# The last stage of a decoder layer on one core: row sums a tile ahead, variance on ScalarE, expert rows landed in 8 KB pieces, fewer rows on TensorE for the first and the last tile

## The chip, the core and the metric

The kernel runs on one core of one Trainium2 chip. The core has a TensorE (PE), a VectorE (DVE), a ScalarE (ACT), a GpSimd (POOL) and a SyncE (SP), which run their own instruction lists side by side and wait for one another through semaphores. The metric is the device time of one launch in microseconds, the median of several runs.

## The reference, cut to what matters

The reference is one decoder layer over 512 prompt tokens and 64 sample tokens (576 in all), with 1024 channels: attention and a gated convolution, a mixture of 64 experts of which each token uses 6, and a per-layer embedding term. The change touches only its last two steps, the sum of a token's six expert rows and the second layer norm:

```
y = jax.ops.segment_sum(yb * row_w[:, None].astype(yb.dtype), row_tok, num_segments=t + 1)
...
h = layer_norm(DN_ALPHA * h + ffn.reshape(n, s, D_MODEL) + ple, lw['ln2_g'], lw['ln2_b'])

def layer_norm(x, g, b):
    mu = jnp.mean(xf, axis=-1, keepdims=True)
    xc = xf - mu
    var = jnp.mean(xc * xc, axis=-1, keepdims=True)
    return (xc * lax.rsqrt(var + LN_EPS) * g + b).astype(x.dtype)
```

## The kernel before

Everything is float32. The 576 tokens are five tiles: tiles 0 to 3 hold 128 prompt tokens each, on 128 partitions, and tile 4 holds the 64 sample tokens. After the projections, attention and routing, a loop over 32 pairs of experts (L1336 to L1344) runs gate, up and down products on PE while SP loads the next pair's weights, each 1 MB load in pieces of 8 KB (L553). Each pass writes its weighted rows to a table in HBM, `expert_rows`, where token i has eight row slots of 4 KB, the first six in use (POOL L695). The shared expert, the residual and the embedding term are already in `res`, in SBUF.

The last stage starts when POOL signals `all_out`, after the last rows have been written.

- **SP** (L613 to L623) issues five loads, `part[t] <- expert_rows` (L617), one for each tile in the order 4, 0, 1, 2, 3 (`LAST_ORDER`); a token's six rows are 24 KB in one run. Then it waits for each tile's `y_done` and stores the tile (L622). All these are on SP's one queue.
- **PE** (L1346 to L1356) sums the first `N_ON_PE = 4` of the six rows of each tile by multiplying them with an identity matrix: four products for each half of 512 channels, accumulated in PSUM. Each product is two matmul instructions in the trace, so a tile is 16 of them.
- **DVE** (L1886 to L1905) waits for the tile's rows, adds the other two rows to `res` (L1893), waits for PE's sum (`part_sum`, L1895) and adds it (L1897), takes the statistics of the two halves (L1900) and joins them (L1902). Then, before it turns to the next tile, it normalises the tile before: `normalise` (L1575 to L1584) takes a reciprocal and makes two passes over the tile, (x - mean) * gain (L1580) and * 1/std + shift (L1583). The second one signals `y_done`.
- **ACT** takes only the square root of the variance (`root`, L846), on a 128x1 column.

The order is written out by hand: nothing plans or reorders it. `normalise` and `root` serve the first layer norm too, and are not changed.

Of the kernel before, what the change touches and what calls it, by code (L numbers as in the profile page):

```python
# [7 lines left out]
F32 = mybir.dt.float32  # L8
# [4 lines left out]
ALU = mybir.AluOpType  # L13
ACT = mybir.ActivationFunctionType
AX = mybir.AxisListType

P = 128
D = 1024
# [5 lines left out]
NT = (T + P - 1) // P  # L24
# [7 lines left out]
NE, TOPK, NGRP, TOPG = 64, 6, 8, 4  # L32
# [26 lines left out]
GATE_SLOT = (1, 0, 0, 0)  # L59
TPAIR = 3  # L60
LAST_ORDER = (NT - 1, *range(NT - 1))
N_ON_PE = 4

def pack_constants():
# [43 lines left out]
def decoder_step(nc, x_prompt, x_sample, p_prompt, p_sample, win_k, win_v, conv_state, w_in, sinks,  # L109
# [4 lines left out]
    with ctx:  # L114
        base0 = (nc.sbuf_base + 31) // 32 * 32

        def at(name, shape, dt, off):
            return nc.alloc_sbuf_tensor_at(name, shape, dt, offset=base0 + off)
# [53 lines left out]
        ident = sm("ident", [P, P], F32)  # L172
# [19 lines left out]
        eps = sm("eps", [P, 1], F32)  # L192
        mv = sm("mv", [P, NT, 2], F32)
        rstd = sm("rstd", [P, NT], F32)
# [7 lines left out]
        stats = at("stats", [P, NT, 4, 6], F32, o_stats)  # L202
# [36 lines left out]
        o_w2, o_w1, o_w0, o_x = 20480, 69632, 118784, 167936  # L239

        res = at("res", [P, NT, D], F32, o_a)
# [68 lines left out]
        g2b2 = at("g2b2", [P, 2, D], F32, o_x)  # L310
# [17 lines left out]
        x2_d = nc.dram_tensor("x2_rows", [T, D], F32)  # L328

        rows_d = nc.dram_tensor("expert_rows", [T * 8 + 1, D], F32)  # L330
        part = [at(f"part{t}", [P, TOPK, D], F32, o_w2 + 4 * TOPK * D * t) for t in range(NT)]

        def sum_banks(n):

            return (proj, att)[n // 2 % 2][:, n % 2 * 2:n % 2 * 2 + 2, :]
# [26 lines left out]
        std_ready, var_ready, x2_ready, x2_out = (sem(n) for n in ("std_ready", "var_ready", "x2_ready", "x2_out"))  # L362
# [15 lines left out]
        part_in = [sem(f"part_in{t}") for t in range(NT)]  # L378
        y_free, all_out, part_sum, part_added = (sem(n) for n in ("y_free", "all_out", "part_sum", "part_added"))
        y_done, y_out = sem("y_done"), sem("y_out")  # L380
# [12 lines left out]
        def ntok(t):  # L393
            return P if t < NT - 1 else NS
# [55 lines left out]
        def _(sp):  # L450
# [14 lines left out]
            for n in range(1, G_AO):  # L465
# [3 lines left out]
                else:  # L469
                    j = Q_AT.index(n)  # L470
# [31 lines left out]
            with sp.Fori(0, 2) as it:  # L502
                for i in range(6):
                    c0 = (COL_CC, COL_CH, COL_CB)[i % 3] + i // 3 * GW
# [32 lines left out]
            for t in range(NT):  # L537
                w = ntok(t)
# [75 lines left out]
            for t in LAST_ORDER:  # L614
                w = ntok(t)
                rows = rows_d[t * P * 8:(t * P + w) * 8, :].rearrange("(p j) n -> p j n", j=8)
                sp.dma_start(part[t][0:w, :, :], rows[:, 0:TOPK, :]).then_inc(part_in[t], 16)  # L617
            for n, t in enumerate(LAST_ORDER):
                w = ntok(t)
                sp.wait_ge(y_done, n + 1)  # L620
# [87 lines left out]
        def _(act):  # L708
# [8 lines left out]
            for n, (t, c) in enumerate(QUADS):  # L717
                act.wait_ge(tr_x, n + 1)
                w = ntok(t)
# [26 lines left out]
            for n in range(N_STEP + 3):  # L746
                if n < N_STEP:
                    j, blk, pair = at_step(n)
                    r = n % 2
                    act.wait_ge(nm_ready, n + 1)  # L750
                    for e in range(2):
                        nc.scalar.activation(s_p[n % 4][:, e, :], s_p[n % 4][:, e, :], ACT.Exp,
                                             bias=nm[:, r, e:e + 1], accum_out=sm_p[:, r, e:e + 1])
# [16 lines left out]
                if n >= 4 and n % 2 == 0:  # L770
                    b = n // 2 - 2
                    j, blk, _ = at_step(2 * b)
# [70 lines left out]
            def root(t):  # L843

                w = ntok(t)
                nc.scalar.activation(rstd[0:w, t:t + 1], mv[0:w, t, 1:2], ACT.Sqrt, bias=eps[0:w, :]).then_inc(std_ready, 1)  # L846
# [5 lines left out]
            for t in range(NT):  # L852
                w = ntok(t)
                for c in range(2):
                    n = 2 * t + c
# [3 lines left out]
                for c in range(2):  # L859
                    n = 2 * t + c  # L860
# [80 lines left out]
                passes(it + 5)  # L941

            for n, t in enumerate(LAST_ORDER):
                act.wait_ge(var_ready, NT + n + 1)
                root(t)

        @block.tensor
        def _(pe):
# [25 lines left out]
            for n, (t, c) in enumerate(QUADS):  # L975
# [3 lines left out]
                w = ntok(t)  # L979
                for j in range(4):  # L980
                    k = 4 * c + j
                    last = nc.tensor.transpose(att[:, n % 4, j * P:j * P + w], x_tok[0:w, t, k * P:(k + 1) * P],
                                               ident[0:w, 0:w])
# [7 lines left out]
            for t in range(NT):  # L991
                w = ntok(t)
# [3 lines left out]
            for b in range(NB_S):  # L996
                last = nc.tensor.transpose(att[:, 2 + b // 4, b % 4 * P:(b % 4 + 1) * P], cache_k[:, b, :], ident[:, :])
# [33 lines left out]
            for n in range(N_STEP + 2):  # L1031
                if n < 24:
                    fill(2)
                if 24 <= n < N_STEP:
# [6 lines left out]
                    for e in range(2):  # L1041
                        r = slice(e * HD, (e + 1) * HD)
                        o = att[r, b % 2, 256:256 + KEYS_S]
                        nc.tensor.matmul(o[:, 0:WIN], q_smp[r, b, :], cache_kt[r, b, :], start=True, stop=True)
                        last = nc.tensor.matmul(o[:, WIN:KEYS_S], q_smp[r, b, :], k_t[r, WIN + SEQ:], start=True, stop=True)
                    last.then_inc(sl_ready, 1)
                if n < N_STEP:
                    j, blk, pair = at_step(n)
# [5 lines left out]
                    for e in range(2):  # L1054
                        r = slice(e * HD, (e + 1) * HD)
# [32 lines left out]
            for b in range(NB_S):  # L1088
                for e in range(2):
                    r = slice(e * HD, (e + 1) * HD)  # L1090
# [48 lines left out]
            for t in range(NT):  # L1139
                w = ntok(t)  # L1140
# [23 lines left out]
            for t in range(NT):  # L1164
                w = ntok(t)
# [180 lines left out]
            for n, t in enumerate(LAST_ORDER):  # L1346
                w = ntok(t)
                pe.wait_ge(part_in[t], 16)
                if n >= 4:
                    pe.wait_ge(part_added, n - 3)  # L1350
                for half in range(2):
                    for j in range(N_ON_PE):
                        last = nc.tensor.matmul(sum_banks(n)[0:w, half, :], ident[0:w, 0:w],  # L1353
                                                part[t][0:w, j, half * 512:(half + 1) * 512],
                                                start=(j == 0), stop=(j == N_ON_PE - 1))
                last.then_inc(part_sum, 1)  # L1356

# [1 line left out]
        def _(dve):  # L1360
# [214 lines left out]
            def normalise(t, gb):  # L1575

                w = ntok(t)
                nc.vector.reciprocal(rstd[0:w, t:t + 1], rstd[0:w, t:t + 1])
                dve.drain()
                nc.vector.scalar_tensor_tensor(res[0:w, t, :], res[0:w, t, :], mv[0:w, t, 0:1], gb[0:w, 0, :],  # L1580
                                               ALU.subtract, ALU.mult)
                dve.drain()
                return nc.vector.scalar_tensor_tensor(res[0:w, t, :], res[0:w, t, :], rstd[0:w, t:t + 1], gb[0:w, 1, :],  # L1583
                                                      ALU.mult, ALU.add)  # L1584
# [299 lines left out]
                passes(it + 5)  # L1884

            dve.wait_ge(ld_ln2, 32)  # L1886
            for n in range(NT + 1):
                if n < NT:
                    t = LAST_ORDER[n]
                    w = ntok(t)  # L1890
                    dve.wait_ge(part_in[t], 16)
                    for j in range(N_ON_PE, TOPK):
                        nc.vector.tensor_tensor(res[0:w, t, :], res[0:w, t, :], part[t][0:w, j, :], ALU.add)  # L1893
                        dve.drain()
                    dve.wait_ge(part_sum, n + 1)  # L1895
                    r = res[0:w, t, :].rearrange("p (a n) -> p a n", a=2)
                    nc.vector.tensor_tensor(r, r, sum_banks(n)[0:w, :, :], ALU.add).then_inc(part_added, 1)  # L1897
                    dve.drain()
                    for c in range(2):
                        nc.vector.bn_stats(stats[0:w, t, c, :], res[0:w, t, c * 512:(c + 1) * 512])  # L1900
                    dve.drain()
                    nc.vector.bn_aggr(mv[0:w, t, :], stats[0:w, t, 0:2, :]).then_inc(var_ready, 1)  # L1902
                if n >= 1:
                    dve.wait_ge(std_ready, NT + n)
                    normalise(LAST_ORDER[n - 1], g2b2).then_inc(y_done, 1)  # L1905

# [24 lines left out]
```

## Time and profile before

| | us |
|---|---|
| median of 3 runs (1363.01 to 1366.27) | 1364.27 |
| the profiled execution's own time | 1364.62 |
| its span, first to last record | 1362.8 |
| PE busy in the span | 1252.1 (92%) |
| DVE busy | 499.0 (37%) |
| last expert pass's last product on PE ends | 1288.2 |
| SP issues the first load of the last stage | 1293.67 |
| DVE's last instruction ends | 1359.73 |

The times in a trace are microseconds from the start of the span. "PE" rows are matmuls, "PEld" their weight loads. A share of busy time is an average over stages: PE is busy for 92% of the span, but in the last 75 us the work passes from DMA to PE to DVE, and only what is late in that stretch matters to this change. The granted clock is TensorE's: 1.00 is 2.4 GHz and 0.50 is 1.2 GHz.

### The profile page before, as it was taken

The page shows a single profiled execution, that of the slowest core. Times are in us where ns is not written, and L with a number is a line of the kernel's source. Part 1 is how long each engine was busy: PE and PEld are TensorE (multiplying, and loading weights), DVE is VectorE, ACT ScalarE, POOL GpSimd, SP SyncE. Part 2 cuts the span into 40 slices and gives each one's busy share as a digit, 9 for nine tenths or more (in the row PEclk, how much of TensorE's full clock was granted, in tenths as well). Part 3 has the DMA queues.
Part 4 walks back from the last instruction along what each step waited for, and adds up shares of the span by engine and source line. Part 5 has one row for each costly group of instructions (what it writes and reads, how often), then busy time and mean ns, then how long its engine had stood idle before and what let it go on. Part 6 is the DMA issues. An engine that isn't in the chain of part 4 may idle for free.

```text
span 1362.8 us, 23702 instructions
## 1 busy us (share of the span) xinstructions
PE 1252.1 (92%) x8911; PEld 1008.6 (74%) x8912; DVE 499.0 (37%) x1090; ACT 298.9 (22%) x547; POOL 129.9 (10%) x200
## 2 busy tenths in 40 slices
PE   6999997999999999999889899989998799999675
PEld 6988876999999999998867667656665466666422
DVE  3455672324444233576862222111111111111128
ACT  3344452212212222224001111111111111111100
POOL 0200000000000000004000111111221121112100
PEclk8999996999999999999899999999999999999968
DMA  8211210222222231433346988999999999999592
GB/s 259 78 52 63 59 36 19 74 94 76 79 92 64 93 98 66 170 104 139 124 197 260 415 318 329 419 421 421 420 419 412 416 414 411 414 408 416 208 376 110
DMA packets 98318, 308.08 MB, mean 226 GB/s; under 512 B 11370, under 2 KB 62402, under 8 KB 73092
## 3 DMA queue, kind: packets, MB, share of 16 engines
q1 hardware_dynamic: 84692, 275.20, 53.0%
q0 software_dynamic: 12480, 28.60, 5.4%
q10 hardware_dynamic: 1088, 3.47, 0.7%
q8 instruction: 40, 0.66, 0.2%
q14 instruction: 18, 0.15, 0.0%
HBM read 295.95 MB, written 26.94 MB: 237 GB/s over the span
## 4 chain that ended last, share of the span: by engine, by line
PE 53%; DMA 35%; DVE 8%; DVEq 1%; issue 1%; ACT 1%; SPq 0%; ACTq 0%; POOLq 0%
DMA w_exp<-in_w_e_down_dram 33%; PE proj L963 31%; PE proj L1124 4%; PE att L1256 3%; PE att L1312 2%; PE att L1133 2%; PE proj L1329 2%; PE proj L1353 2%; PE att L1056 1%; DMA pg_raw<-in_w_ple_gate_dram 1%; PE att L1018 1%; PE att L1124 1%; PE att L1069 1%; DMA part<-expert_rows 1%; PE att L1092 0%
## 5 line engine op out<-in xcount | busy, mean ns | idle before, releaser
L1312 PE MATMUL att<-w_exp,xt 128*64 128x256 f32 x2560 | 289.4, 383 | 23.2 <-issue 11.3
L1312 PEld LDWEIGHTS att<-w_exp,xt 128*64 128x64 f32 x2560 | 221.0, 138 | 100.1 <-issue 46.1
L963 PE MATMUL proj<-h_hi,w_hi 128*128 128x288 f32 x800 | 178.3, 305 | 4.8 <-DVE h_lo L1365 4.8
L963 PE MATMUL proj<-h_lo,w_hi 128*128 128x288 f32 x800 | 171.9, 297 | 0.0
L963 PE MATMUL proj<-h_hi,w_lo 128*128 128x288 f32 x800 | 171.8, 297 | 0.0
L1329 PE MATMUL proj<-w_exp,ht_e 128*64 128x512 f32 x640 | 149.2, 607 | 11.2 <-DMA w_exp<-in_w_e_down_dram 6.6
L963 PEld LDWEIGHTS proj<-h_hi,w_hi 128*128 128x128 f32 x800 | 128.4, 190 | 20.2 <-issue 15.2
L963 PEld LDWEIGHTS proj<-h_lo,w_hi 128*128 128x128 f32 x800 | 129.7, 190 | 0.0
L963 PEld LDWEIGHTS proj<-h_hi,w_lo 128*128 128x128 f32 x800 | 129.4, 190 | 0.0
L432 DVE TENSOR_TENSOR w_lo<-w_raw,w_hi 128x2048 fp32r<-128x2048 f32 x33 | 75.6, 2291 | 100.1 <-ACT w_hi L422 94.7
L1329 PEld LDWEIGHTS proj<-w_exp,ht_e 128*64 128x64 f32 x640 | 51.1, 139 | 81.8 <-issue 80.0
L422 ACT ACTIVATE w_hi<-w_raw 128x2048 fp32r<-128x2048 f32 x33 | 63.0, 1909 | 97.6 <-PE proj L963 80.8
L1857 DVE TENSOR_SCALAR ysb<-proj,tabw 128x512 f32 x40 | 30.0, 751 | 144.1 <-PE proj L1329 144.1
L1848 DVE TENSOR_TENSOR sg<-sg,att 128x256 f32<-128x256 f32 x40 | 16.8, 421 | 121.7 <-ACT sg L918 121.7
L1852 DVE TENSOR_TENSOR h_e<-sg,att 128x256 f32<-128x256 f32 x40 | 16.8, 421 | 120.0 <-PE att L1312 119.8
L925 ACT ACTIVATE ysb<-proj,tabw 128x512 f32 x40 | 27.5, 687 | 145.2 <-PE proj L1329 145.2
L963 PE MATMUL proj<-mix_hi,w_hi 128*128 128x288 f32 x256 | 55.7, 300 | 1.7 <-DVE mix_lo L1483 1.7
L963 PE MATMUL proj<-mix_hi,w_lo 128*128 128x288 f32 x256 | 55.3, 298 | 0.0
L963 PE MATMUL proj<-mix_lo,w_hi 128*128 128x288 f32 x256 | 55.3, 298 | 0.0
L920 ACT ACTIVATE ht_e<-att 128x256 f32<-128x256 f32 x40 | 15.3, 383 | 181.9 <-PE att L1318 181.9
L1266 PEld LDWEIGHTS proj<-ident,xg 128*128 128x128 f32 x328 | 43.5, 195 | 15.7 <-issue 14.6
L1266 PE MATMUL proj<-ident,xg 128*128 128x128 f32 x328 | 54.3, 289 | 0.1
(338 smaller groups left out, 1744.8 us busy)
## 6 DMA issues: line engine op xcount, KB each, us to landing
w_exp<-in_w_e_gate_dram SPq DMA_DIRECT2D x64, 1024.0 KB, 17.1
w_exp<-in_w_e_up_dram SPq DMA_DIRECT2D x64, 1024.0 KB, 17.4
w_exp<-in_w_e_down_dram SPq DMA_DIRECT2D x64, 1024.0 KB, 17.2
w_raw<-in_w_in_dram SPq DMA_DIRECT2D x21, 1024.0 KB
part<-expert_rows SPq DMA_DIRECT2D x4, 3072.0 KB, 27.2
w_raw<-in_w_in_dram SPq DMA_DIRECT2D x8, 512.0 KB
w_raw<-in_w_attn_out_dram SPq DMA_DIRECT2D x8, 512.0 KB
w_raw<-in_w_conv_out_dram SPq DMA_DIRECT2D x4, 1024.0 KB
```

What stands on the lines that cost most here:

```text
L422: nc.scalar.activation(w_hi[:, g.par, :], w_raw[:, g.par, :], ACT.Copy).then_inc(hi_done, 1)
L432: nc.vector.tensor_tensor(w_lo[:, g.par, :], w_raw[:, g.par, :], w_hi[:, g.par, :].bitcast(F32), ALU.subtract).then_inc(w_ready, 1)
L925: nc.scalar.activation(ysb[:, bass.ds(side_of, 1), 0:512].rearrange("p o n -> p (o n)"), proj[:, 2, :], ACT.Copy, scale=tabw[:, bass.ds(k, ...
L963: last = nc.tensor.matmul(proj[:, 2 * i + a, 0:HALF], lhs, x[:, c, a * HALF:(a + 1) * HALF], start=(c == 0 and n == 0), stop=(c == KC - 1 ...
L1124: last = nc.tensor.matmul(out, x[:, c, t * P:t * P + w], v[:, c, :], start=(c == 0 and n == 0), stop=(c == KC - 1 and n == 2))
L1133: last = nc.tensor.matmul(out, x[:, c, t * P:t * P + w], v[:, c, half * 512:(half + 1) * 512], start=(c == 0 and n == 0), stop=(c == 1 and ...
L1256: last = nc.tensor.matmul(gate_bank(u)[0:w, :], x[:, c, t * P:t * P + w], v[:, c, :], start=(c == 0 and n == 0), stop=(c == KC - 1 and n = ...
L1266: last = nc.tensor.transpose(proj[:, half, c * P:(c + 1) * P], xg[:, :, half * 4 + c], ident[:, :])
L1312: last = nc.tensor.matmul(att[e * SLOT:(e + 1) * SLOT, m, 0:FF], xt[:, c, e * SLOT:(e + 1) * SLOT], weights[e][:, c, :], start=(c == 0), s ...
L1329: last = nc.tensor.matmul(proj[e * SLOT:(e + 1) * SLOT, 2 + half, :], ht_e[:, c, e * SLOT:(e + 1) * SLOT], down[e][:, c, half * 512:(half ...
L1353: last = nc.tensor.matmul(sum_banks(n)[0:w, half, :], ident[0:w, 0:w], part[t][0:w, j, half * 512:(half + 1) * 512], start=(j == 0), stop= ...
L1857: nc.vector.tensor_scalar(ysb[:, bass.ds(side_of, 1), 512:D].rearrange("p o n -> p (o n)"), proj[:, 3, :], tabw[:, bass.ds(k, 1)], None, A ...
```

## The change

Four things are changed, all in the last stage.

1. `N_ON_PE` becomes a count for each place in the order, `(2, 4, 4, 4, 3)`: PE sums two rows of tile 4 and three of tile 3, and DVE adds the other four and three.
2. The rows are laid out in SBUF as three pairs of rows with 32 unused bytes behind each pair, so that each partition's 24 KB is landed in three pieces of 8 KB.
3. DVE's order: it adds its rows of tile n + 1 (`add_rows`) before it waits for PE's sum of tile n (`add_sum`), and normalises tile n - 1 (`last_norm`) after that. The pass that adds PE's sum is now a `tensor_tensor_reduce`, which also gives the sum over channels, and a 128x1 multiplication makes it minus the mean. The statistics passes are gone.
4. ACT computes the sum of (x - mean)^2 over channels with a `Square` activation and an accumulator (its elements go to the place of the tile's first row), then the root with a scale of 1/1024.

```
-N_ON_PE = 4
+N_ON_PE = (2, 4, 4, 4, 3)
...
-        part = [at(f"part{t}", [P, TOPK, D], F32, o_w2 + 4 * TOPK * D * t) for t in range(NT)]
+        part = [at(f"part{t}", [P, TOPK // 2, 2 * D + 8], F32, o_w2 + 4 * TOPK // 2 * (2 * D + 8) * t) for t in range(NT)]
...
-                sp.dma_start(part[t][0:w, :, :], rows[:, 0:TOPK, :]).then_inc(part_in[t], 16)
+                sp.dma_start(part[t][0:w, :, 0:2 * D],
+                             rows[:, 0:TOPK, :].rearrange("p (i j) n -> p i (j n)", j=2)).then_inc(part_in[t], 16)
...
                 act.wait_ge(var_ready, NT + n + 1)
-                root(t)
+                nc.scalar.activation(part_row(t, 0), res[0:w, t, :], ACT.Square, bias=mv[0:w, t, 0:1],
+                                     accum_out=mv[0:w, t, 1:2])
+                act.drain()
+                nc.scalar.activation(rstd[0:w, t:t + 1], mv[0:w, t, 1:2], ACT.Sqrt, bias=eps[0:w, :],
+                                     scale=1.0 / D).then_inc(std_ready, 1)
...
+            def add_rows(n):
+                t = LAST_ORDER[n]
+                r = res[0:ntok(t), t, :]
+                dve.wait_ge(part_in[t], 16)
+                for j in range(N_ON_PE[n], TOPK):
+                    nc.vector.tensor_tensor(r, r, part_row(t, j), ALU.add)
+                    dve.drain()
+            def add_sum(n):
+                ...
+                dve.wait_ge(part_sum, n + 1)
+                nc.vector.tensor_tensor_reduce(r, r, sum_banks(n)[0:w, :, :].rearrange("p a n -> p (a n)"), 1.0, 0.0,
+                                               ALU.add, ALU.add, mv[0:w, t, 0:1]).then_inc(part_added, 1)
+                dve.drain()
+                nc.vector.tensor_scalar(mv[0:w, t, 0:1], mv[0:w, t, 0:1], -1.0 / D, None, ALU.mult).then_inc(var_ready, 1)
+            def last_norm(n):
+                ...
+                dve.wait_ge(std_ready, NT + n + 1)
+                nc.vector.reciprocal(rstd[0:w, t:t + 1], rstd[0:w, t:t + 1])
+                nc.vector.scalar_tensor_tensor(r, r, mv[0:w, t, 0:1], g2b2[0:w, 0, :], ALU.add, ALU.mult)
+                dve.drain()
+                nc.vector.scalar_tensor_tensor(r, r, rstd[0:w, t:t + 1], g2b2[0:w, 1, :], ALU.mult, ALU.add).then_inc(y_done, 1)
+            add_rows(0)
+            for n in range(NT):
+                if n + 1 < NT:
+                    add_rows(n + 1)
+                add_sum(n)
+                if n:
+                    last_norm(n - 1)
+            last_norm(NT - 1)
```

## Rows read from the trace of the kernel before

**Rows 1.** The chain of waits from 1293 us on: start, length, what.
```profile
1293.67 10.46 DMA part<-expert_rows
1304.18 22.33 PE proj L1353 x32
```

**Rows 2.** DVE in order of time: start, length, line, operation, shape, count.
```profile
1340.21 2.52 DVE L1893 TENSOR_TENSOR res<-res,part 128x1024 f32<-128x1024 f32 x2
1342.80 1.22 DVE L1897 TENSOR_TENSOR res<-res,att 128x1024 f32<-128x1024 f32 x1
1344.12 1.29 DVE L1900 BATCH_NORM_STATS2 stats<-res 128x6 f32<-128x512 f32 x2
1345.48 0.21 DVE L1902 BATCH_NORM_AGGREGATE mv<-stats 128x2 f32<-128x12 f32 x1
1345.60 0.11 DVE L1578 RECIPROCAL rstd<-rstd 128x1 f32<-128x1 f32 x1
1348.35 2.52 DVE L1893 TENSOR_TENSOR res<-res,part 128x1024 f32<-128x1024 f32 x2
...
1358.45 1.28 DVE L1583 SCALAR_TENSOR_TENSOR res<-res,rstd,g2b 128x1024 f32<-128x1024 f32 x1
```

**Rows 3.** Stretches: length, busy (count) by engine, granted clock, DMA share, GB/s.
```profile
1293.00:1304.18 11.18, 0.00 (x0) 0.00 (x1) 0.00 (x0) 0.00 (x0) 0.00 (x0) 0.52 0.87 207
1304.18:1317.80 13.62, 13.62 (x16) 3.46 (x16) 2.44 (x2) 0.00 (x0) 0.00 (x0) 0.50 0.99 424
1317.80:1320.60 2.80, 2.80 (x4) 1.17 (x4) 2.38 (x3) 0.00 (x0) 0.00 (x0) 0.50 1.06 456
1320.60:1326.40 5.80, 5.80 (x15) 2.55 (x14) 2.63 (x4) 0.30 (x1) 0.00 (x0) 0.99 0.98 419
```

**Rows 4.** Groups by line and shape, 1288 to 1363 us: busy, mean ns.
```profile
L1353 PE MATMUL att<-part,ident 128*128 128x512 f32 x32 | 13.9, 592 | 0.0
```

**Rows 5.** Loads of the last stage: issues, and time to landing for each pair of issues.
```profile
L617 SPq DMA_DIRECT2D part<-expert_rows x5: 432/532/618, 1293.7 to 1296.0; - x5
DMA to landing us min/median/max: 10.5/13.8/17.1
DMA to landing us min/median/max: 23.8/27.2/30.6
DMA to landing us min/median/max: 30.6/34.5/38.5
```

**Rows 6.** Stretches, columns as in rows 3: the last stage's landings and the expert loop.
```profile
1304.20:1311.30 7.10, 7.10 (x9) 2.08 (x10) 2.44 (x2) 0.00 (x0) 0.00 (x0) 0.50 0.94 405
1332.00:1334.50 2.50, 2.50 (x8) 1.06 (x7) 2.42 (x3) 0.00 (x0) 0.00 (x0) 1.00 0.50 115
1000.00:1200.00 200.00, 184.37 (x1344) 120.11 (x1344) 34.28 (x60) 30.76 (x60) 36.50 (x60) 0.99 1.01 414
```

**Rows 7.** Stretches at the kernel's start, where loads are in 1 KB pieces.
```profile
18.54:23.70 5.16, 5.16 (x21) 5.16 (x22) 2.85 (x6) 0.00 (x0) 0.00 (x0) 0.50 1.12 300
23.70:30.00 6.30, 6.30 (x50) 6.30 (x49) 0.00 (x0) 0.65 (x1) 0.00 (x0) 1.00 1.01 286
```

**Rows 8.** DVE groups by line and shape: the reduce form, its accumulator read, a plain addition.
```profile
L1421 DVE CUSTOM_DVE_ANT_0 s_p<-att,mask_p 128x256 f32<-128x256 f32 x64 | 24.6, 423 | 45.6 <-PE att L1056 45.6
L1421 DVE DVE_READ_ACCUMULATOR2_ANT mx<- 128x1 f32 x64 | 5.3, 84 | 0.0
L1852 DVE TENSOR_TENSOR h_e<-sg,att 128x256 f32<-128x256 f32 x40 | 16.8, 421 | 120.0 <-PE att L1312 119.8 <-issue 0.2
```

**Rows 9.** ACT groups by line and shape, whole span.
```profile
L752 ACT ACTIVATION_READ_ACCUMULATOR s_p<-s_p,nm 128x1 f32 x64 | 11.9, 187 | 0.0
L419 ACT ACTIVATE w_hi<-w_raw 128x1024 fp32r<-128x1024 f32 x8 | 8.0, 1046 | 7.0 <-PE proj L963 5.8 <-DMA w_raw<-in_w_in_dram 1.2
L846 ACT ACT_TABLE_LOAD x2 | 2.6, 1283 | 0.0
L846 ACT ACTIVATE rstd<-mv,eps 128x1 f32<-128x1 f32 x8 | 2.4, 295 | 44.1 <-DVE mv L1902 31.7 <-DVE mv L1624 12.5
```

More of the change, by code:

```diff
@@ L330, in decoder_step, with part_row @@
         rows_d = nc.dram_tensor("expert_rows", [T * 8 + 1, D], F32)
-        part = [at(f"part{t}", [P, TOPK, D], F32, o_w2 + 4 * TOPK * D * t) for t in range(NT)]
+        part = [at(f"part{t}", [P, TOPK // 2, 2 * D + 8], F32, o_w2 + 4 * TOPK // 2 * (2 * D + 8) * t) for t in range(NT)]
+        def part_row(t, j, half=None):
+            c0 = j % 2 * D + (half or 0) * 512
+            return part[t][0:ntok(t), j // 2, c0:c0 + (D if half is None else 512)]
         def sum_banks(n):
@@ L943, in _ @@
             for n, t in enumerate(LAST_ORDER):
+                w = ntok(t)
                 act.wait_ge(var_ready, NT + n + 1)
-                root(t)
+                nc.scalar.activation(part_row(t, 0), res[0:w, t, :], ACT.Square, bias=mv[0:w, t, 0:1],
[3 more added lines that the diff above has]
+                                     scale=1.0 / D).then_inc(std_ready, 1)
         @block.tensor
@@ L1351, in _ @@
                 for half in range(2):
[L1352 to L1355, printed above, removed]
+                    for j in range(N_ON_PE[n]):
+                        last = nc.tensor.matmul(sum_banks(n)[0:w, half, :], ident[0:w, 0:w], part_row(t, j, half),
+                                                start=(j == 0), stop=(j == N_ON_PE[n] - 1))
                 last.then_inc(part_sum, 1)
@@ L1886, in _ @@
             dve.wait_ge(ld_ln2, 32)
[L1887 to L1897, printed above, removed]
-                    dve.drain()
[L1899 to L1905, printed above, removed]
+            def add_rows(n):
[4 more added lines that the diff above has]
+                    nc.vector.tensor_tensor(r, r, part_row(t, j), ALU.add)
+                    dve.drain()
@@ new lines, in add_sum @@
+            def add_sum(n):
+                t = LAST_ORDER[n]
+                w = ntok(t)
+                r = res[0:w, t, :]
+                dve.wait_ge(part_sum, n + 1)
[3 more added lines that the diff above has]
+                nc.vector.tensor_scalar(mv[0:w, t, 0:1], mv[0:w, t, 0:1], -1.0 / D, None, ALU.mult).then_inc(var_ready, 1)
@@ new lines, in last_norm @@
+            def last_norm(n):
+                t = LAST_ORDER[n]
+                w = ntok(t)
+                r = res[0:w, t, :]
+                dve.wait_ge(std_ready, NT + n + 1)
[3 more added lines that the diff above has]
+                nc.vector.scalar_tensor_tensor(r, r, rstd[0:w, t:t + 1], g2b2[0:w, 1, :], ALU.mult, ALU.add).then_inc(y_done, 1)
```

## Prediction

> **What bounds the kernel now.** I read the chain of waits first, then DVE in order of time, then tables of stretches for PE's clock and the landings. The chain's last 70 us lie wholly in the stage that the change touches: it waits 10.5 us for tile 4's rows, then stands on PE for 22.3 us until 1326.5 [rows 1], and from there it is DVE alone. The reader is to see three limits one behind the other.
>
> PE is first. Tile 4's 16 matmuls fill 1304.18 to 1317.80 at a granted clock of 0.50 (1.2 GHz), 0.85 us each; tile 0's begin at 1317.80 and the clock is at 0.99 to 1.00 (2.4 GHz) from 1320.6 [rows 3]. Then a matmul takes 0.43 us (32 in 13.9 us) [rows 4], 6.9 us for a tile of 16.
>
> The landings are second. Five loads are issued 1293.7 to 1296.0, 0.58 us apart, and land 10.5, 17.1, 23.8, 30.6 and 38.5 us after their issue [rows 5]: tile 4 at L4 = 1304.2, tile 0 at L0 = 1311.3, tile 1 at L1 = 1318.6, tile 2 at L2 = 1326.0, tile 3 at L3 = 1334.5. Before 1304.2 the core's DMA moves 207 GB/s, after it 405 to 456 [rows 3, 6]; in the last 2.5 us before L3 only 115 [rows 6].
>
> DVE is third. Its period is 1348.35 - 1340.21 = 8.14 us for a tile [rows 2]: two row additions 2.59 (1.295 each with the gap behind), PE's sum 1.32, statistics and their join 1.36 + 0.12, and a normalise of 2.75. DVE never catches up with the landings after 1326.5, and it ends at 1358.45 + 1.28 = 1359.73. The last store and the end of the span take another 1362.8 - 1359.73 = 3.07 us.
>
> **PE.** Two rows of tile 4 are 8 matmuls at 0.85 us: 1304.2 to 1311.0 instead of 1317.8. PE then waits for L0, 0.3 us. Tile 0's 16 begin at 1311.4. What its clock does there I take from two places. Between 1304.18 and 1317.80 PE was full of 64x64 products and the clock stayed at 0.50; it rose 2.8 us after the first 128x128 ones [rows 3]. At the kernel's start 128x128 products ran 5.2 us at 0.50 before it rose [rows 7]. So the rise comes 2.8 to 5.2 us into tile 0, at 1314 to 1317; if the 64x64 ones count after all, at 1320.6 as before. Tile 0 is done at 1320 by the first, and by the second at 1311.4 + 9.2 (10.8 matmuls) + 5.2 x 0.43 = 1322.9. Tile 1 follows in 6.9 us, by 1327 to 1330; tile 2 (after L2) by 1334 to 1337; tile 3's 12 matmuls take 5.2 us after L3, by 1339.7 to 1342.
>
> **DVE, each step's price.** Row additions: four for tile 4 5.2 us, two for tiles 0 to 2 2.6, three for tile 3 3.9 [rows 2]. The new sum pass: its form ran at 423 ns for 128x256 where a plain addition took 421, plus an accumulator read of 84 ns [rows 8]; so 1.32 + 0.08, and a 128x1 multiplication priced as the reciprocal (0.11) with a 0.08 gap: 1.6 us. Bounds: 1.4, if the small ones overlap, and 1.9. The last normalise: 2.75, as now. Per tile 2.6 + 1.6 + 2.75 = 6.95 against 8.14.
>
> **ACT.** Square over 128x1024: the copy of that shape took 1046 ns, the accumulator read 187, the root 295 [rows 9]; with 0.2 for a drain and hops 1.7 us (bounds 1.5 and 2.0). It lies beside work: for tiles 4 to 2 at least a normalise and a sum (4.3 us) stand between a tile's sum and its own normalise, for tile 3 one normalise, 2.75. So it costs nothing, with 1.0 us to spare at the tightest place.
>
> **The 8 KB pieces.** The load of tile 4 is not shown in pieces. The nearest rows: the expert weights, landed in 8 KB pieces, moved 414 GB/s over 200 us [rows 6]; the last stage's 24 KB pieces 405 to 456 [rows 3, 6]; 1 KB pieces at the kernel's start 300 [rows 7]. Tiles 0 to 3 are 12.58 MB: 30.4 us at 414 against 30.3 now, so L3 stays; at 300 it would be 41.9 us, 11.6 later; at 456, the best stretch, 27.6, 2.7 earlier. I take 414, its own size, and leave every L where it is. Issuing takes SP 0.43 to 0.62 us a load now [rows 5]; more descriptors may add a few tenths, only the first of which is on the path.
>
> The 64-partition load runs at half the rate of the others with DMA 0.87 busy [rows 3]. The Trainium skill, "DMA: Bandwidth & Descriptors", section "The descriptor swizzle", has a 128-partition load write half its SBUF ports from partitions 0 to 63 and half from 64 to 127; by that rule a load of 64 partitions has half the ports whatever its pieces, and L4 stays. If the rule were wrong for this and smaller pieces ran it at the full rate, L4 and all behind it would come some 3.8 us earlier.
>
> **The sum.** DVE now:
> - rows of tile 4: 1304.2 to 1309.4; rows of tile 0: L0 1311.4 to 1314.0; sum 4: to 1315.6
> - rows of tile 1: L1 1318.7 to 1321.3; sum 0 (PE 1320 to 1322.9): to 1322.9 to 1324.5; norm 4: to 1325.7 to 1327.3
> - rows of tile 2: L2 1326.0, to 1328.7 to 1329.9; sum 1: to 1330.3 to 1331.6; norm 0: to 1333.1 to 1334.4
> - rows of tile 3: L3 1334.5, to 1338.4; sum 2: 1340.0; norm 1: 1342.8; sum 3 (PE 1339.7 to 1342): 1344.4; norm 2: 1347.1; norm 3: 1349.9
>
> With either clock DVE is waiting when tile 3 lands, so the end is L3 + 3.9 + 2 x 1.6 + 3 x 2.75 = L3 + 15.4 = 1349.9. That is 9.8 us before 1359.73. The store behind stays 3.07. The profiled execution took 1364.62, so the changed kernel would take 1354.8; the median of the runs is 0.35 below that execution: **1354.5**. Where the 9.8 comes from: PE's late start is gone (it had held DVE back to 1326.5), and of 1.2 us a tile saved on DVE most is then spent waiting for L2 and L3. What is late next is the last landing.
>
> **Rivals.**
> - *The clock is late.* If it rises 16.4 us after the first 128x128 product (the distance from 1304.18 to 1320.6) at 1327.8, tile 0 on PE ends at 1325.1, sum 0 and all behind it follow, rows of tile 3 start at 1336.4 and DVE ends at 1352.6: +2.7, 1357.2. For it: the first stretch in rows 3. Against: the short rise in rows 7.
> - *The clock never rises: the other side.* PE streams only identity products here, with waits for landings possible between tiles. At 0.85 us the 60 matmuls of the last four tiles (16 + 16 + 16 + 12) run from 1311.4 to 1362.7; then sum 3, norm 2 and norm 3, 7.1 us, and 3.07: 1372.9 in span, 1374.4, 10 us slower. It decides from the rise on: c us at 0.50 put PE's end at 1337.2 + 0.5 c, which costs something above c = 11 and makes the kernel slower than before above c = 31, a rise after 1342. Against: before, the same 128x128 products got 1.00 from 1320.6 to the end.
> - *Square and Sqrt do not share ACT's table.* Then two loads of 1.28 us [rows 9] come in each tile, ACT needs 4.3 us, and the last normalise waits 1.5: 1356.0. Copies and sigmoids alternate in the expert loop without loads, and the span has 6 loads in all, but no Square runs in it. The Trainium skill, "ScalarE: Activation LUTs", section "Table sets: the hidden batching unit", says that cheap functions are in every set as filler and does not name Square among its examples. By its price of a switch, 2.66 us with the drain, two switches a tile would hold up the last two normalises, and an estimate from that page is 1361.4.
> - *Landings come earlier* (tail or first tile, above): DVE's own chain from sum 0 at 1321.3 then ends at 1348.2, or all shifts by up to 3.8: 1351 to 1353.
> - *8 KB pieces land later*: each us of L3 costs one; 2 us, 1356.5; at 300 GB/s 11.6 us, 1366, no gain.
>
> **How the numbers follow.** Forecast 0.66, late clock 0.08, no clock 0.04, tables 0.06, earlier landings 0.09, later landings 0.07 (0.03 of it by so much that the gain is gone). A change of 0.2% (2.7 us) is about what a measurement can tell from none. The forecast's own range is 1353 to 1357 (0.3 us more or less in each of five sums and row additions). Taking in earlier landings, tables and the late clock gives 1351 to 1359. Faster 0.92; same 0.03; slower 0.05, the cold clock and the lower rate of landing.
>
> **What would show it.** PE's first tile is 8 matmuls and ends near 1311, and the granted clock is 1.00 before 1321. The reduce form takes about 1.22 us for 128x1024, each accumulator read under 0.2. DVE's idle time in front of the row additions is put down to the DMA, about 1.4 us for tile 3, and from there to its end it has no idle time over 0.2 us. Landings are within 1 us of those above. ACT shows one table load in the stage, or none, and its root ends before DVE asks. I am wrong if DVE waits for PE's sum after tile 0, if it waits for ACT at the end, or if L3 + 15.4 isn't its end.

## The result and the profile after

The changed kernel takes 1353.46 us (median of 4 runs, 1353.21 to 1353.84) against 1364.41 for the kernel before beside it; the ratio is 0.9919, 95% interval 0.9902 to 0.9936. The prediction was 1354.5, range 1351 to 1359. Its profiled execution took 1353.30 us, with a span of 1351.5.

The kernel's time varies from run to run by more than the effects looked for below (33 runs of the kernel before on one chip went from 1356.9 to 1368.8). Much of that lies ahead of the last stage: in the traces the stage begins anywhere between 1290.89 and 1296.73, while two traces of the changed kernel agree on the stage's own length to 0.14 us. So the main measure here is **the stage**: from the start of SP's first load of expert rows to the end of DVE's last instruction, both from the trace. Before it was 1359.73 - 1293.67 = 66.06 us [rows 2], and the pieces of the span's 11.3 us are:

| | before | after | difference |
|---|---|---|---|
| start of the stage | 1293.67 | 1291.28 | -2.39 |
| the stage | 66.06 | 56.16 | -9.90 |
| end of DVE to end of span | 3.07 | 4.06 | +0.99 |

The last row is the last store. It landed 2.6 us after its issue before the change and 3.6 after it:

```profile
out_dram<-res SPq DMA_DIRECT2D x1, 512.0 KB, 2.6
out_dram<-res SPq DMA_DIRECT2D x1, 512.0 KB, 3.6
```

A second trace of the changed kernel has 3.6 again, so this is no spread of the runs. From its first load to the end of the span the change is worth 69.1 - 60.2 = 8.9 us, not 9.9. Why the store takes longer is open.

First DVE of the changed kernel, in order of time; columns as in rows 2.

```profile
1302.42 5.09 DVE L1903 TENSOR_TENSOR res<-res,part 64x1024 f32<-64x1024 f32 x4 [15.56 <-DMA part<-expert_rows]
...
1316.95 2.53 DVE L1903 TENSOR_TENSOR res<-res,part 128x1024 f32<-128x1024 f32 x2 [3.29 <-DMA part<-expert_rows]
1319.60 1.22 DVE L1912 CUSTOM_DVE_ANT_0 res<-res,proj 128x1024 f32<-128x1024 f32 x1
...
1324.41 2.52 DVE L1903 TENSOR_TENSOR res<-res,part 128x1024 f32<-128x1024 f32 x2 [0.73 <-DMA part<-expert_rows]
...
1332.81 3.82 DVE L1903 TENSOR_TENSOR res<-res,part 128x1024 f32<-128x1024 f32 x3 [1.67 <-DMA part<-expert_rows]
1336.75 1.22 DVE L1912 CUSTOM_DVE_ANT_0 res<-res,att 128x1024 f32<-128x1024 f32 x1
1337.89 0.08 DVE L1912 DVE_READ_ACCUMULATOR2_ANT mv<- 128x1 f32 x1
1338.07 0.15 DVE L1915 TENSOR_SCALAR mv<-mv 128x1 f32<-128x1 f32 x1
1338.14 0.15 DVE L1923 RECIPROCAL rstd<-rstd 128x1 f32<-128x1 f32 x1
...
1340.76 1.21 DVE L1912 CUSTOM_DVE_ANT_0 res<-res,proj 128x1024 f32<-128x1024 f32 x1
...
1346.16 1.28 DVE L1926 SCALAR_TENSOR_TENSOR res<-res,rstd,g2b 128x1024 f32<-128x1024 f32 x1
```

The reader is to see what stands in the brackets. Every wait of DVE in the stage is for `part<-expert_rows`, none for PE; before, DVE's waits in this stage were 15.0 us for the first landing and 14.5 for PE. From 1332.81, tile 3's landing, DVE runs without a gap to 1347.44.

Then PE, in stretches of its clock (columns as in rows 3).

```profile
1302.36:1309.20 6.84, 6.84 (x8) 1.65 (x8) 4.87 (x4) 0.00 (x0) 0.00 (x0) 0.50 1.01 422
1309.40:1315.10 5.70, 5.57 (x8) 2.43 (x8) 3.82 (x5) 1.35 (x3) 0.00 (x0) 0.50 1.01 424
1315.30:1319.00 3.70, 3.70 (x10) 1.55 (x9) 1.97 (x2) 1.27 (x2) 0.00 (x0) 0.99 1.01 421
```

Tile 4 is 8 matmuls at 1.2 GHz, and the clock is up 5.8 us after tile 0's first 128x128 product. PE is done with tile 0 at 1319.0, 27.7 us into the stage; before it was at 1326.4, 32.7.

The loads, issues and times to landing (all five together):

```profile
L622 SPq DMA_DIRECT2D part<-expert_rows x5: 488/664/6043, 1291.3 to 1294.1; - x5
DMA to landing us min/median/max: 11.0/24.3/38.7
```

Tile 4 lands 11.1 us after the first issue and tile 3 at 41.5, against 10.5 and 40.8 before. One issue, that of tile 3, the last of the five, now holds SP for 6.0 us; SP's next work is the first store, at 1323.7, so nothing waits behind it. Last, ACT:

```profile
1313.70 1.15 ACT L952 ACTIVATE part<-res,mv 64x1024 f32<-64x1024 f32 x1 [26.97 <-DVE mv L1915]
1314.75 0.19 ACT L952 ACTIVATION_READ_ACCUMULATOR part<-res,mv 64x1 f32 x1
1314.99 1.28 ACT L955 ACT_TABLE_LOAD   x1
1316.29 0.30 ACT L955 ACTIVATE rstd<-mv,eps 64x1 f32<-64x1 f32 x1
...
1342.26 1.15 ACT L952 ACTIVATE part<-res,mv 128x1024 f32<-128x1024 f32 x1 [2.39 <-DVE mv L1915]
1343.32 0.19 ACT L952 ACTIVATION_READ_ACCUMULATOR part<-res,mv 128x1 f32 x1
1343.57 0.30 ACT L955 ACTIVATE rstd<-mv,eps 128x1 f32<-128x1 f32 x1
```

There is one table load, between the first Square and the first root, and none later. The last root ends at 1343.87, 0.9 us before DVE asks for it.

### The profile page after: what moved, and what is told of

The parts are those of the page before. It is cut to its first block, busy times and chain, and to the rows that moved or that the text cites. A ratio compares the mean times of both kernels' runs of the same rounds, so it can differ in the third digit from the quotient of the medians.

```text
span 1351.5 us, 23684 instructions
## 1 busy us (share of the span) xinstructions
PE 1246.7 (92%) x8899; PEld 1008.8 (75%) x8900; DVE 495.9 (37%) x1088; ACT 305.4 (23%) x557; POOL 129.9 (10%) x200
## 4 chain that ended last, share of the span: by engine, by line
PE 51%; DMA 38%; DVE 7%; DVEq 1%; issue 1%; ACT 1%; SPq 0%; ACTq 0%; POOLq 0%
DMA w_exp<-in_w_e_down_dram 33%; PE proj L974 31%; PE proj L1135 4%; PE att L1267 3%; DMA part<-expert_rows 3%; PE att L1323 2%; PE att L1144 2%; PE proj L1340 2%; PE att L1067 1%; DMA pg_raw<-in_w_ple_gate_dram 1%; PE att L1029 1%; PE att L1080 1%; PE att L1135 1%; PE att L1104 0%; PE att L1103 0%
## 5 line engine op out<-in xcount | busy, mean ns | idle before, releaser
L1323 PE MATMUL att<-w_exp,xt 128*64 128x256 f32 x2560 | 289.1, 383 | 23.3 <-issue 11.3
L926 ACT ACTIVATE ht_e<-att 128x256 f32<-128x256 f32 x40 | 15.4, 384 | 181.8 <-PE att L1329 181.8
L974 PE MATMUL proj<-mix_hi,w_lo 128*128 128x288 f32 x256 | 55.6, 299 | 0.0
```

The lines of the kernel that those rows point to most:

```text
L974: last = nc.tensor.matmul(proj[:, 2 * i + a, 0:HALF], lhs, x[:, c, a * HALF:(a + 1) * HALF], start=(c == 0 and n == 0), stop=(c == KC - 1 ...
L1323: last = nc.tensor.matmul(att[e * SLOT:(e + 1) * SLOT, m, 0:FF], xt[:, c, e * SLOT:(e + 1) * SLOT], weights[e][:, c, :], start=(c == 0), s ...
```

## The experiments

"Stage" is read from each kernel's trace, and "rest" is what follows it to the end of the span; "median" is the difference of medians from the kernel before on the same chip.

| kernel | stage, us | expected | rest | median |
|---|---|---|---|---|
| before | 66.06 | | 3.1 | |
| as changed, shown above | 56.16 | | 4.1 | -10.95 |
| `a0_after`, as changed again | 56.30 | 56.2 | 4.1 | -9.53 |
| `b1_split`, before + rows on PE (2, 4, 4, 4, 3) | 62.18 | 61.3 | 3.1 | -4.70 |
| `b2_warm`, before + PE kept at full clock | 58.69 | 57.3 | 3.1 | -7.56 |
| `a1_pieces24`, 24 KB pieces | 55.50 | 55.4 to 55.6 | 4.0 | -10.11 |
| `a2_all4`, four rows of each tile on PE | 61.65 | 60.6 | 3.1 | -4.76 |
| `a3_order`, old order on DVE | 56.36 | 56.7 | 4.0 | -9.76 |
| `a4_stats`, statistics on DVE | 59.26 | 58.9 | 3.1 | -6.24 |
| `c2_ports`, tile 4 in two halves, two queues | 58.53 | 52.7 | 3.1 | -7.47 |
| `c1_last4_24`, 24 KB, four rows of tile 3 on PE | 54.90 | 54.7 | 3.1 | -10.17 |
| `c4_warm24`, 24 KB, unused products on PE | 55.46 | 55.5 | 4.0 | -10.77 |
| `c5_mid`, tile 4 on partitions 32 to 95 | 53.50 | 51.4 | 3.1 | -12.10 |
| `c6_best`, the same, PE's share cut | 52.23 | 51.7 | 3.1 | -17.62 |

The rest is 4.0 to 4.1 us, with a last store of 3.6, in five of these traces and 3.1, with one of 2.6, in the others. Where two kernels differ in it, the end of the span moves by 1 us more or less than the stage: against the kernel as changed, `a2_all4` is then 4.5 us worse and `a4_stats` 2.1, and `c1_last4_24` is 1.5 us better than `a1_pieces24`. No run tells what the five have in common.

### What held the stage before

`b1_split` is one part of the change alone on the kernel before.

```
-N_ON_PE = 4
+N_ON_PE = (2, 4, 4, 4, 3)
```

> The kernel before with one part of the change alone: PE sums 2, 4, 4, 4, 3 rows instead of 4 of each tile. Call the stage the time from SP's first load of expert rows to the end of DVE's last instruction: 66.06 us before, 56.16 after the change. Theory (the stage before was late because PE spent 13.7 us on tile 4 at 1.2 GHz and began tile 0 that late): PE ends tile 4 at 17.4 us of the stage and tile 0 at about 27.3 instead of 32.7, DVE then runs without a wait at 8.14 us a tile plus 1.3 for the third row of tile 3: stage 61.3 us, 4.8 less. Rival (PE's split matters little, the order and the variance on ScalarE carry the gain): stage 65 or more.

Stage 62.18, 3.9 less; ratio 0.9970 (0.9949 to 0.9990). DVE waited 6.0 us for PE instead of 14.5, and then ran at 8.14 us a tile to the end, as the theory has it. The 0.9 us over the expectation are mostly the first landing, 11.3 us after the issue instead of 10.5.

`b2_warm` leaves the kernel before alone but for unused products, ahead of PE's wait for tile 4:

```
+            pe.wait_ge(ld_ln2, 32)
+            for i in range(18):
+                nc.tensor.matmul(att[:, 3, :], ident[:, :], g2b2[:, i % 2, 0:512], start=True, stop=True)
             for n, t in enumerate(LAST_ORDER):
```

> The kernel before, with nothing changed but 18 products of 128x512 with the identity that PE runs into an unused PSUM bank while it waits for tile 4's rows (their results are not used), so that its clock does not fall. Theory (what held the stage back was the clock, not the number of rows on PE): the granted clock stays at 1.00, tile 4's 16 matmuls take 0.43 us each and end at 17.4 us of the stage, tile 0's at 24.3, and DVE, with the old order and the old statistics, ends at 57.3: 8.8 us less than 66.06, nearly as much as the whole change. Rival A (the 64x64 products of tile 4 let the clock fall whatever came before): tile 4 starts at 0.43 us a matmul and slows down to 0.85, the stage is 59 to 63 us. Rival B (the clock was not the reason): 66.

Stage 58.69, 7.4 less; ratio 0.9954 (0.9931 to 0.9977). The first stretch is the unused products, the second tile 4 and tile 0 on PE:

```profile
1290.00:1305.80 15.80, 15.77 (x38) 6.76 (x36) 0.75 (x1) 1.97 (x2) 1.01 (x1) 1.00 0.64 151
1306.49:1320.60 14.11, 14.11 (x32) 5.01 (x32) 7.44 (x8) 0.29 (x1) 0.00 (x0) 1.00 0.99 421
```

32 matmuls take 14.1 us at 1.00; before, the 16 of tile 4 took 13.6 [rows 3]. With the old split, order and statistics, the clock alone gives three quarters of the change's 9.9 us. Rival A is refuted too: the clock stayed at 1.00 for the 7.0 us that the 64x64 products ran. The 1.4 us missing are in the landings: tile 4's came at 10.9, and tile 1's rows came so late that PE began that tile at 26.5 and DVE waited for it.

### One part undone at a time

`a0_after` is the control.

> The changed kernel as it is, beside the others on the same chip. Expected: a stage (from SP's first load of expert rows to the end of DVE's last instruction) of 56.2 us again and a median 9.9 us below the kernel before. If the start of the stage, at 1291.3 us in the trace after against 1293.7 before, is moved by the change, it starts below 1292 again; if the expert loop only varies from run to run, it starts anywhere from 1291 to 1297.

Stage 56.30, which begins at 1294.14; over all traces the stage begins between 1290.89 and 1296.73. So the 2.4 us by which the shown trace starts the stage earlier are not the change's.

`a1_pieces24` lands a token's rows in one piece:

```
-                sp.dma_start(part[t][0:w, :, 0:2 * D],
-                             rows[:, 0:TOPK, :].rearrange("p (i j) n -> p i (j n)", j=2)).then_inc(part_in[t], 16)
+                sp.dma_start(part[t][0:w, :, :], rows[:, 0:TOPK, :]).then_inc(part_in[t], 16)
```

> The changed kernel with the rows of a token landed in one piece of 24 KB again; all else as changed. Theory (smaller pieces bring nothing here): the landings come 10.5, 17.7, 24.9, 32.3 and 40.8 us after the first issue, as in the kernel before, against 11.1, 18.2, 25.7, 33.1 and 41.5; SP's fourth load is issued in under 1 us instead of 6; the stage is 55.4 to 55.6. Rival (8 KB pieces avoid stragglers at the end): 57 or more.

Stage 55.50: the 8 KB pieces cost 0.7 to 0.8 us, the whole of it in the landings. Tile 4's came 10.4 us after the first issue instead of 11.1, tile 3's 40.9 instead of 41.5 and, in the control, 41.7:

```profile
L622 SPq DMA_DIRECT2D part<-expert_rows x5: 432/496/791, 1290.9 to 1293.4; - x5
DMA to landing us min/median/max: 10.3/23.6/38.4
```

The issue that was held for 6.0 us is the fifth, not the fourth as the expectation has it; here it takes 0.4. The medians (-10.11 against the control's -9.53 on the same chip) are too coarse to show it.

`a2_all4` gives PE four rows of every tile (`N_ON_PE = (4, 4, 4, 4, 4)`).

> The changed kernel with four rows of every tile on PE; all else as changed. Theory: PE spends 13.7 us on tile 4, begins tile 0 at 24.8 us of the stage, the clock rises 2.8 us into it, as before the change, and PE ends tiles 0 to 3 at 33.1, 40, 46.9 and 53.8; DVE waits for each of them: stage 60.6 us, 4.4 more than 56.2. Rival (adding rows a tile ahead hides PE's lateness): 57 or less.

Stage 61.65, 5.4 us more than as changed. The list of DVE's waits in that stage, grouped (us in total, times, longest us):

```profile
DVE res L1903 <- DMA part<-expert_rows: 20.2, 2, 15.6
DVE res L1912 <- PE proj L1364: 12.4, 3, 5.4
DVE res L1912 <- PE att L1364: 0.7, 2, 0.3
```

DVE waits for PE at every tile again, 13.1 us in five waits. The edit also gives PE the fourth row of tile 3, which is a gain where PE is early (`c1_last4_24` below), so the loss is the first tile's. Fewer rows on PE for that tile is thus the part that carries the change: more than half of its 9.9 us go with it.

`a3_order` adds a tile's rows directly before PE's sum of the same tile:

```
-            add_rows(0)
             for n in range(NT):
-                if n + 1 < NT:
-                    add_rows(n + 1)
+                add_rows(n)
                 add_sum(n)
```

> The changed kernel with DVE's order undone: the rows of a tile are added directly before PE's sum of the same tile, as in the kernel before; all else as changed. Theory (with PE early, the order is worth little, since PE's sum of a tile is ready 7 to 10 us after its landing and DVE has other work for most of that): DVE waits for PE at each of the first four tiles, but the stage is only 0.5 us longer, 56.7. Rival (working a tile ahead is what hides PE's sums): 59 or more.

Stage 56.36, within 0.2 us of the two traces of the kernel as changed. DVE waits 2.0 us for PE at tile 4 and 6.1 at tile 0 (where it otherwise waits for landings), and after that only 0.3 at tiles 1 and 2. Working a tile ahead brings nothing measurable once PE is early.

`a4_stats` returns the statistics to DVE:

```
-                nc.vector.tensor_tensor_reduce(r, r, sum_banks(n)[...], 1.0, 0.0, ALU.add, ALU.add, mv[0:w, t, 0:1])
-                nc.vector.tensor_scalar(mv[0:w, t, 0:1], mv[0:w, t, 0:1], -1.0 / D, None, ALU.mult)
+                nc.vector.tensor_tensor(r, r, sum_banks(n)[...], ALU.add)
+                for c in range(2):
+                    nc.vector.bn_stats(stats[0:w, t, c, :], res[0:w, t, c * 512:(c + 1) * 512])
+                nc.vector.bn_aggr(mv[0:w, t, :], stats[0:w, t, 0:2, :])
...
-                nc.scalar.activation(part_row(t, 0), res[0:w, t, :], ACT.Square, ...)
+                root(t)
```

> The changed kernel with the statistics back on DVE (two statistics passes and their join) and only the root on ScalarE; all else as changed. Theory: each tile costs DVE 1.35 us more; the waits for the landings of tiles 2 and 3 (0.7 and 1.7 us) swallow what is added before them, and the two tiles whose sums come after the last landing cost 2.7: stage 58.9 us. Rival (the landing sets the end and ScalarE's part is just as long): 56.5 or less. Second rival (all five tiles pay): 62.9.

Stage 59.26, 3.0 more: the two tiles summed after the last landing pay in full, the others mostly in time that DVE would have waited.

### Where the stage ends now, and a faster version

`c4_warm24` adds the 18 unused products, which are to keep the clock up, to the kernel with 24 KB pieces.

> The changed kernel with 24 KB pieces and the 18 unused products that keep PE's clock at 1.00 while it waits for tile 4. Theory (after the change the clock no longer matters, since the landings hold DVE back): PE ends tile 0 by 24.5 us of the stage instead of 27, DVE's waits for the landings stay, stage 55.5 us as without them. Rival (the late clock still costs): 54.5 or less.

Stage 55.46 against 55.50, but the run did not do what it was for: the clock was up for tile 4 alone. PE did tile 4's 8 matmuls in 3.64 us at 1.00 and then waited 3.4 us for tile 0, and 2.6 us into that wait the clock fell. Tile 0 began at 0.50:

```profile
1303.39:1307.03 3.64, 3.64 (x8) 0.98 (x8) 3.44 (x3) 0.00 (x0) 0.00 (x0) 1.00 1.01 432
1310.47:1315.80 5.33, 5.33 (x7) 2.23 (x8) 3.79 (x5) 1.21 (x2) 0.00 (x0) 0.50 1.02 432
```

PE ended tile 0 27.6 us into the stage, not by 24.5 as expected, and in `a1_pieces24` at 27.2. What the run shows is that PE's being done with tile 4 three microseconds earlier is worth nothing. That a warm clock on tile 0 would be worth nothing either is argued, from the waits: in `a1_pieces24`, in this run and in both traces of the kernel as changed, DVE never waits for PE, and tile 3's landing, 40.8 to 41.7 us into the stage, is the last thing that it waits for.

`c1_last4_24` is `N_ON_PE = (2, 4, 4, 4, 4)` on 24 KB pieces.

> The changed kernel with 24 KB pieces, and PE sums four rows of tile 3 instead of three. Theory (from the last landing on the path is DVE's row additions and three normalises; PE's 16 matmuls end 6.9 us after the landing and DVE asks for them at 6.6): one row addition of 1.3 us goes and 0.5 of it comes back as a wait for PE: stage 54.7 us, against 55.5 with 24 KB pieces alone. Rival (PE is then the limit): 55.5 or more.

Stage 54.90: one row addition less behind the last landing, and 0.8 us of waiting for PE. Three rows of tile 3 on PE, as the change has it, is 0.6 us worse than four.

`c2_ports`, on 24 KB pieces, was to speed up the first load by using all partitions. PE sums three rows of tile 4 (`N_ON_PE = (3, 4, 4, 4, 3)`), from the upper half:

```
+                j0 = N_ON_PE[0] if t == NT - 1 else 0
+                sp.dma_start(part[t][0:w, j0:TOPK, :], rows[:, j0:TOPK, :]).then_inc(part_in[t], 16)
...
+            act.dma_start(part[NT - 1][NS:P, 0:N_ON_PE[0], :], rows[:, 0:N_ON_PE[0], :]).then_inc(part_pe, 16)
```

> Built on the changed kernel with 24 KB pieces: of tile 4's six rows, three go to partitions 0 to 63 (DVE adds them) from SP's queue, and three to partitions 64 to 127 (PE sums them) from ScalarE's queue, at the same time. Theory (tile 4's load runs at 207 GB/s because it writes to 64 partitions only): both parts have landed by 7.5 us of the stage instead of 11, the later tiles land 3 to 3.6 us earlier, tile 3 at 37.2 to 37.8. PE then is the limit for DVE, since its clock rises late: stage 52.7 us. Rival (the first load is slow because the queue starts up or for its source, and where it lands does not matter): landings as in the kernel with 24 KB pieces, stage 55.5 or more.

A miss: stage 58.53. Time to landing from both queues, issued at the same moment:

```profile
part<-expert_rows SPq DMA_DIRECT2D x1, 768.0 KB, 6.3
part<-expert_rows ACTq DMA_DIRECT2D x1, 768.0 KB, 13.6
```

SP's half lands at 6.3, but ACT's, which PE needs, at 13.6, beside SP's next tile, and tile 0 at 18.2, no earlier than before. Two stretches, up to the first landing and up to the second, moved 188 and 271 GB/s:

```profile
1294.17:1300.50 6.33, 0.00 (x0) 0.00 (x0) 0.00 (x0) 0.00 (x0) 0.00 (x0) 0.50 0.85 188
1300.50:1307.80 7.30, 0.00 (x0) 0.00 (x0) 3.65 (x3) 0.00 (x0) 0.00 (x0) 0.50 0.97 271
```

Either the partitions were not the reason or the two halves still met on the same ports. `c5_mid` tells these apart with one queue and one load, to the middle partitions. It has 24 KB pieces and 14 unused products ahead of tile 4, and DVE zeroes the other partitions of that buffer, which PE reads too:

```
+                p0 = 32 if t == NT - 1 else 0
+                sp.dma_start(part[t][p0:p0 + w, :, :], rows[:, 0:TOPK, :]).then_inc(part_in[t], 16)
...
+                        lhs = ident[:, :] if n else ident[:, 32:32 + NS]
...
-N_ON_PE = (2, 4, 4, 4, 3)
+N_ON_PE = (6, 4, 4, 4, 4)
```

> Built on the changed kernel with 24 KB pieces. Tile 4's six rows are landed by one load as before, but on partitions 32 to 95 instead of 0 to 63, and PE sums all six (its identity columns are shifted by 32; DVE sets partitions 0 to 31 and 96 to 127 of that buffer to zero while it is idle). PE sums four rows of each other tile, tile 3 too, and 14 unused products keep its clock up while it waits. 
Landings of `c5_mid`:

```profile
DMA to landing us min/median/max: 6.3/21.0/35.8
```

The stretch up to the first landing, in `c5_mid` and then in `a1_pieces24`:

```profile
1291.85:1298.10 6.25, 6.25 (x16) 2.66 (x14) 4.93 (x2) 0.00 (x0) 0.00 (x0) 1.00 0.83 315
```

```profile
1290.89:1301.25 10.36, 0.00 (x0) 0.00 (x0) 0.00 (x0) 0.00 (x0) 0.00 (x0) 0.50 0.89 204
```

The same 1.57 MB land in 6.3 us instead of 10.3, at 315 GB/s with the start of the load in it instead of 204; tile 3 lands at 38.1. The unused products are not the reason: in `c4_warm24`, which has 18 of them, tile 4 lands at 10.5. So where 64 rows are written decides. The Trainium skill, "DMA: Bandwidth & Descriptors", section "The descriptor swizzle", which for a load of 128 partitions has 0 to 63 and 64 to 127 on different ports, agrees with it; which engines met on a port in `c2_ports` no trace shows, and that part stays argued. The stage, 53.50, missed its 51.4: PE began tile 4 only at 8.6, after DVE had zeroed the other partitions in two instructions of 5.2 us, and DVE waited 2.0 us for PE at tile 3. Against `c1_last4_24`, the nearest kernel with tile 4 on partitions 0 to 63, it is 1.4 us less.

`c6_best` changes that to `N_ON_PE = (6, 3, 3, 4, 4)`.

> The kernel that lands tile 4 on partitions 32 to 95, with PE's share cut where PE was late: 6 rows of tile 4, 3 of tiles 0 and 1, 4 of tiles 2 and 3. Theory (in that kernel PE began tile 4 at 8.6 us of the stage, after DVE's zeroing, had 88 matmuls to do and ended tile 3 at 46.8, where DVE waited 2.0 us for it): 80 matmuls, PE ready for tile 3 when it lands at 38.1 and done at 45.0, DVE's row additions of tiles 0 and 1 lie in its waits for landings: stage 51.7 us against 53.5. Rival (DVE, with two more row additions, becomes the limit before tile 3 lands): 53 or more.

```profile
1331.72 2.52 DVE L1913 TENSOR_TENSOR res<-res,part 128x1024 f32<-128x1024 f32 x2 [1.34 <-DMA part<-expert_rows]
...
1338.91 1.22 DVE L1922 CUSTOM_DVE_ANT_0 res<-res,proj 128x1024 f32<-128x1024 f32 x1 [0.46 <-PE proj L1372]
```

Stage 52.23, 3.9 us less than the kernel as changed; DVE waits 1.3 us for the last landing, 0.5 for PE behind it, and 1.6 for PE at tile 4. Ratio to the kernel before 0.9872 (0.9853 to 0.9891), median 1348.77 against 1366.39. The profiled executions differ by 13.9 us, and so do the stages (13.8); the other 3.8 of the medians' 17.6 lie in runs without a trace, and the spread (1343.3 to 1350.8) is wide enough for them. It is the fastest here.

## Why the prediction was right

**The size.** Predicted 9.8 us less in the stage, measured 9.90 and, in the control, 9.76. The predicted 1354.5 is 1.0 us over the median, and that closeness is in part luck: the stage of the profiled execution began 2.4 us earlier, which is not the change's, and its last store landed 1.0 us later, which the prediction had left as it was (3.07 us, measured 4.06).

**PE.** Eight matmuls from the first landing, at 0.85 us: as predicted (6.84 us). The clock's rise was put 2.8 to 5.2 us into tile 0, and came at 5.8; that changed nothing, as the sum had it that DVE waits for tile 3 with either. `b1_split`, `b2_warm` and `a2_all4` show that PE's late, slow start was what held the kernel before. That it no longer does stands in DVE's waits, none of which is for PE; no run kept PE's clock up through tile 0 of the changed kernel with all else left as it was.

**DVE's prices.** The reduce form took 1.22 us for 128x1024, the accumulator read 0.08: as priced. Sum and mean together were 1.4 us, not 1.6, because the small instructions overlap, and the normalise 2.62 instead of 2.75. From tile 3's landing to DVE's end it was 14.6 us instead of 15.4.

**The landings** are the term that was mis-sized the other way: L3 was left at its place for 8 KB pieces and came 0.7 us later; `a1_pieces24` gives 0.7 to 0.8 back. The two errors, -0.8 and +0.7, cancel by luck.

**What is late next** was named as the last landing, with a wait of about 1.4 us for tile 3. It was 1.67, and every wait of DVE in the stage was for a landing.

**Credit.** The text expected most of the 1.2 us a tile saved on DVE to be lost in waits for landings. `a4_stats` shows 3.0 us kept in the stage, about half of what five tiles save. The prediction gave the reordering no price of its own; `a3_order` shows it to be 0.1 to 0.2 us. `b1_split` (3.9) and `a2_all4` (5.4) differ for the same edit, it seems because what it frees is worth more where DVE is faster.

**The rivals.** The late clock did not come: the rival put the rise 16.4 us after the first 128x128 product and it was 5.8, and the clock did rise, which settles the other side too. (The rival's own sum leaves out a wait of 1.2 us for PE at tile 1; with it DVE ends at 1353.0, not 1352.6.) Later landings came, by 0.7 us, at the price that the rival gives, one for one. Square ran before the root's table was loaded and after, without a load of its own, so the tables' rival is refuted. Of earlier landings, the mechanism was real, but 8 KB pieces don't touch it: it needed other partitions, and `c5_mid` had tile 4 4.1 us and tile 3 2.8 us earlier.

## What to carry to other kernels

Before work is moved off an engine that is late, look at the clock it was granted while it was late: here 18 products that nobody reads gave 7.4 us, three quarters of what four edits gave. Where a stage begins with a load and PE waits for it until its clock is down, give PE little to do for the first tile, or keep the clock up; with it up, `c6_best` has PE sum all six rows of that tile. Then count from the last landing forward: what stands behind it on the busiest engine is the end, and moving one addition there to an idle engine was worth more here (0.6 us) than a reordering ahead of it (0.1 to 0.2). Check in the trace that a change meant to hold the clock did hold it: in `c4_warm24` it did so for one tile, and the time alone would not have told. With a spread of 10 us from run to run, a difference of 1 us can be read only in the trace, from a fixed event to another.

## What the runs showed of the hardware

- 64x64 float32 products never raised the granted clock in these traces: 13.6 us of them back to back stayed at 0.50, in the kernel before as in `a2_all4`, and the clock rose only after 128x128 products had begun (2.8 us before the change, 5.8 after, and between these or up to 6.0 in every other trace where PE began at 0.50). Yet in `b2_warm` a clock that was at 1.00 stayed there for the 7 us that 64x64 products ran. In `c4_warm24`, after 3.6 us of them, it fell 2.6 us into a wait.
- A load of 64 rows of 24 KB took 10.3 us to partitions 0 to 63 and 6.3 us to partitions 32 to 95.
- Pieces of 8 KB instead of 24 KB made the landings 0.7 to 1.0 us later and held SP for 6.0 us at the fifth issue. What held it no run shows.
- In `b2_warm`, `c4_warm24`, `c5_mid` and `c6_best`, which run unused products on PE, tile 1 landed late: 26.2 us after the first issue in `c4_warm24` against 24.8 in `a1_pieces24`, and 8.6 us behind tile 0 in `c5_mid`, against 7.3 in `a1_pieces24`. Tile 3 was not late for it (40.8 and 40.9). Why is open.
- The last store of 512 KB landed 3.6 us after its issue in five traces and 2.6 in nine. Why is open.
